# Attention units on one core: the transposes of a unit placed ahead of the product of the unit before it

## What is computed

```python
s = jnp.einsum('bqhd,bkhd->bhqk', qb, k) * scale
p = masked_softmax(s, pos[None, :] <= t[:, None])
return jnp.einsum('bhqk,bkhd->bqhd', p.astype(dt), v)
```

## Time and profile before

| | |
|---|---|
| median of 3 runs | 4166.8 us (4161.8 to 4168.43) |
| profiled execution | 4173.57 us, its span 4171.8 us |
| PE busy | 3686.4 us, 88% of the span |
| PEld busy | 2947.4 us, 71% |
| DVE busy | 2156.1 us, 52% |
| POOL busy | 1802.5 us, 43% |
| ACT busy | 1407.6 us, 34% |
| MLA, first layer | 248 to 306 us of the span |
| NSA, first layer | 346 to 450 us |
| Sparse, first layer of the second stack | 2494 to 2553 us |
| Fox, first layer of the second stack | 2553 to 2614 us |
| granted TensorE clock, mean | 0.905 of full speed |

### The profile page before, as it was taken

How to read it: one execution, slowest core, us unless ns; L and a number is a source line. 1 busy time by engine, 2 the same in 40 slices (tenths; PEclk the granted TensorE clock), 3 DMA queues, 4 the chain that set the end, 5 groups by cost and what they waited for, 6 DMA issues and landing times. The chain is left out here.

```text
span 4171.8 us, 48813 instructions
## 1 busy us (share of the span) xinstructions
PE 3686.4 (88%) x16148; PEld 2947.4 (71%) x16156; DVE 2156.1 (52%) x3077; ACT 1407.6 (34%) x2442; POOL 1802.5 (43%) x976
## 2 busy tenths in 40 slices
PE   7888899999888889999997778999998778999997
PEld 6755786787776657877786556877877566877876
DVE  4255497212243565962123475447863465547863
ACT  3234323322232352333222225323333225323332
POOL 3137553444340564443442447434543447434542
PEclk9877999999997689999998888999998888999998
DMA  3200122223321002222242110622233110622233
GB/s 117 71 11 1 61 96 76 85 96 131 123 77 65 0 1 81 90 81 86 89 144 101 51 61 1 242 81 81 96 131 110 49 61 1 242 81 84 97 136 116
DMA packets 99596, 354.89 MB, mean 85 GB/s; under 512 B 11888, under 2 KB 12528, under 8 KB 99312
## 3 DMA queue, kind: packets, MB, share of 16 engines
q1 hardware_dynamic: 99440, 352.94, 25.1%
HBM read 350.73 MB, written 2.10 MB: 85 GB/s over the span
## 5 line engine op out<-in xcount | busy, mean ns | idle before, releaser
L201 POOL TENSOR_TENSOR weights_lo<-arena,weights_hi 128x1024 fp32r<-128x1024 f32 x504 | 1288.5, 2558 | 1840.9 <-ACT weights_hi L195 1840.9
L263 PE MATMUL ps<-moving_hi,weights_hi 128*128 128x512 f32 x2752 | 720.7, 406 | 96.1 <-ACT weights_hi L195 38.0
L195 ACT ACTIVATE weights_hi<-arena 128x1024 fp32r<-128x1024 f32 x522 | 548.6, 1053 | 720.4 <-PE ps L414 403.2
L263 PE MATMUL ps<-moving_lo,weights_hi 128*128 128x512 f32 x2752 | 692.0, 393 | 2.4 <-DVE moving_lo L218 1.2
L263 PEld LDWEIGHTS ps<-moving_hi,weights_hi 128*128 128x128 f32 x2752 | 532.3, 194 | 223.5 <-issue 50.7
L263 PE MATMUL ps<-moving_hi,weights_lo 128*128 128x512 f32 x2752 | 686.0, 392 | 0.0
L263 PEld LDWEIGHTS ps<-moving_lo,weights_hi 128*128 128x128 f32 x2752 | 524.2, 190 | 117.9 <-DVE moving_lo L218 5.8
L263 PEld LDWEIGHTS ps<-moving_hi,weights_lo 128*128 128x128 f32 x2752 | 522.1, 190 | 109.6
L802 POOL TENSOR_SCALAR arena<-arena 128x128 f32<-128x128 f32 (+1 forms) x320 | 344.9, 1095 | 297.7 <-DVE arena L724 232.8
L1689 DVE SCALAR_TENSOR_TENSOR arena<-arena 128x1024 f32<-128x1024 f32 x128 | 188.3, 1483 | 421.5 <-DMA arena<-modw_first 344.7
L1573 DVE SCALAR_TENSOR_TENSOR arena<-arena 128x512 f32<-128x512 f32 x240 | 258.0, 1150 | 0.0
(11 more groups left out here) (298 smaller groups left out, 4542.9 us busy)
## 6 DMA issues: line engine op xcount, KB each, us to landing
arena<-wstream SPq DMA_DIRECT2D x532, 512.0 KB, 3.3
arena<-modw_first SPq DMA_DIRECT2D x64, 512.0 KB, 4.1
arena<-modw SPq DMA_DIRECT2D x64, 512.0 KB, 5.2
arena<-xT SPq DMA_DIRECT2D x1, 2048.0 KB, 8.7
outT<-arena SPq DMA_DIRECT2D x1, 2048.0 KB, 7.0
arena<-con SPq DMA_DIRECT2D x1, 1411.5 KB, 11.3
arena<-par SPq DMA_DIRECT2D x4, 136.0 KB, 3.1
arena<-arena SPq DMA_DIRECT2D x32, 2.0 KB, 1.7
```

What stands on the lines that cost most here:

```text
L195: m.nc.scalar.activation(m.w_hi[:, j % 2, :], slab(m, base + j), ACT.Copy).then_inc(hi_ready, 1)
L201: m.nc.gpsimd.tensor_tensor(m.w_lo[:, j % 2, :], slab(m, base + j), m.w_hi[:, j % 2, :].bitcast(F32), ALU.subtract)\
L263: mm = m.nc.tensor.matmul(bank, unit_tile(w, k), a[:, k, :], start=(p == 0 and k == 0), stop=(p == 2 and k == KD - 1))
```

## The change

In each round, TensorE's list now has the transposes of unit u between the scores of unit u+1 and the product of unit u-1. Before, they stood behind that product. No instruction is added or taken away, and the orders of the other engines are the same. It holds for all four kinds of attention.

```diff
--- before.py
+++ after.py
@@ -692,9 +692,9 @@
             for u in range(NU):
                 if u + 1 < NU:
                     score(u + 1)
+                turn(u)
                 if u:
                     product(u - 1)
-                turn(u)
             product(NU - 1)
```

## The result

The changed kernel takes 4266.61 us (median of four runs, 4263.66 to 4269.82) against 4164.3 for the kernel before (four runs, 4158.29 to 4168.43). The ratio is 1.0247, 95% interval 1.0229 to 1.0265: 102 us slower, where 100 was forecast. The span of the profiled execution went from 4171.8 to 4268.0.

The account below looks back on a forecast made before the run. ScalarE and VectorE handing over to each other bound the kernel (GpSimd in Sparse). Longer rings and stage ends +77 us and NSA's lower clock +23 gave +100, 4267 us, chance 0.48; own range 4250 to 4285, 8 in 10 4232 to 4302.

Parts of the forecast that it names:

- The ring of ScalarE and VectorE: In MLA before the change, ScalarE and VectorE waiting on each other set the pace, 5.82 us a unit; NSA 5.67.
- The new ring: After the change, a two-unit loop through scaling, transposes, product and ScalarE's copies: 12.95 us in MLA, 13.49 in NSA.
- The clock in NSA: Transposes and product of even NSA units run at the lower clock: +1.9 us a pair, +11.5 a stage.
- The ends: MLA's end: product(6) delays the last high parts by 2.1 to 3.8 us, a slow last product adds 1.1; +4.2 taken.
- Sparse: Sparse stage: the two-unit loop slightly exceeds GpSimd's pace, and the end costs more; 5 to 8 us, 6.5 taken.
- Fox: Fox stage: same unit as MLA, without weights and with one score term; 7.5 us longer.
- stages outside the attention would keep their lengths: Sign: stages after the attention keep their lengths, no growth.
- The even pace: MLA units come every 6.5 us, with TensorE idle 1.4 us before transposes; in Fox idle 1.4 to 2.2.
- The order does not matter: Rival: scaling always ends before the next unit's scores, so time stays within 8 us; no change, chance 0.04.
- faster: Rival: ScalarE's high copy finds all three transpose banks ready, saving perhaps half of 66.2 us; 4134, chance 0.03.
- The clock holds: Rival: TensorE's clock stays up in NSA and only the rings lengthen: +77 us, 4244; chance 0.20.
- The rival of falls in Sparse and Fox: Rival: the clock also falls about three times in each Sparse and Fox stage, +27 us above forecast, 4294; chance 0.18.

Follow-up runs that it names:

- The two edits on ScalarE: Changed kernel with the half copy behind the high parts: 4236.91 us; with two buffers for high and low parts: 4258.58; with both: 4165.9.
- the scaling runs: GpSimd scaling two of the four query tiles: on the changed kernel 4162.2 us, on the kernel before 4138.72 us.
- the run that makes it hold in NSA: Changed kernel with 11 added identity matmuls ahead of the transposes of every even NSA unit after the first: 4244.74 us.

## Why the prediction was right, point by point

- **What bounds the kernel.** The ring of ScalarE and VectorE, with TensorE and GpSimd outside, was right for the middle of the stages. The run with less scaling and the old order kept 5.8 us a unit. It was incomplete for the beginnings and ends, where GpSimd is on the path.
- **The new ring.** The sum of 12.95 for two units of MLA measured 12.91, and NSA's 13.49 measured 13.18 and 13.31 once the clock was held. The two edits on ScalarE show that it closes over both waits for the product, and the scaling runs show that GpSimd is in it.
- **The clock in NSA.** Idle 3.87 us (at least 3.5), low clock behind it, 1.7 us a pair for the 1.9 estimated. NSA grew by 27.0 and 26.0 for 28.5. That the total comes so near is partly two errors against each other. With the clock held the stages grew by 11.9 and 11.7, where I had 17: the pairs 13.2 to 13.3 and not 13.49, the first two units 0.6 shorter, the end 1.4 and not 2.5 to 4.5 longer. The clock then took 15.1 and 14.3 and not 11.5, since it slowed the end too.
- **The ends.** A rest of 2.1 to 3.8 and a slow last product were named; the last high parts of MLA came 3.6 us later behind their transposes (4.64 against 1.07). In MLA the time from the last reciprocal to the end of the stage grew by 4.2 and 3.6 for the 4.2 forecast, in Fox by 3.0. The run with the last unit alone gave 40 us in the timed runs and 33 in the span, for a range of 17 to 39.
- **Sparse**: 8.3 and 8.0 for 6.5. **Fox**: 4.5 and 4.4 for 7.5. Fox is the term that was mis-sized most. Its pairs did take 12.9 to 13.0 in the steady part, but the last reciprocal came 50.93 after the first matmul of the stage where it had been 49.48, so 1.45 and not 3.3. Its third reciprocal came 1.1 us earlier than before (18.80 after the first matmul instead of 19.89), because TensorE's clock rose 15.2 us after the first matmul there and not 20.1, and the first units follow TensorE. From the third reciprocal to the last it was 2.5 longer, which is the ring.
- **The moved wait hands something on.** I had said that stages outside the attention would keep their lengths. The compressed stage behind MLA grew by 1.7 and 1.9. The stage's stretch has a granted clock of 0.53 before and 0.50 after (the first field behind the five engines; the windows are of unequal length, and the clock is at the upper level only in the first 2.3 us of the first):

```profile
306.00:346.00 40.00, 34.07 (x112) 18.49 (x112) 11.37 (x18) 6.17 (x11) 31.49 (x32) 0.53 0.00 1
```

```profile
317.00:352.00 35.00, 29.47 (x102) 17.93 (x102) 10.20 (x15) 5.33 (x9) 31.15 (x32) 0.50 0.00 1
```

  MLA's last rows are at the lower clock now, and the next stage starts there. It isn't the order in MLA alone: with the new order in NSA only, the second layer's compressed stage took 42.7 us too, behind a MLA in the old order.
- **The even pace.** I had MLA's and Fox's units at an even 6.5 us, with 1.4 us idle on TensorE (in Fox 1.4 to 2.2). The second MLA stage and both Fox stages come near that: 6.1 to 6.8 us, with 1.1 to 1.5 idle. In the first MLA stage the units come in turns of 5.8 to 5.9 and 7.0 to 7.1, with 0.7 and 1.9 to 2.4 idle; the mean of a pair is the same. Nothing hung on it, since in the middle of these stages the clock held all the same.
- **The rivals.** "The order does not matter" and "faster" fell with the result. "The clock holds" gives 4244, and the run that makes it hold in NSA gives 4244.74. It was not what happened, and that the two agree to 1 us is luck: the stages of that run grew by 68 us in sum and not by 77, with NSA 5 a stage under and the compressed stage 2 a stage over. The rival of falls in Sparse and Fox came true in small part: in the first Sparse stage the transposes of units 4, 6 and 7 took 2.4 us, in the second those of 5 and 7, and in both Fox stages those of unit 6. Those of the last two units belong to the ends. That TensorE might run the product before the waiting transposes did not happen. The Trainium skill ("TensorE: Matmul & The Clock Gate", Part 1, on queue depths) says that TensorE's queue can pull weight loads ahead of matmuls in flight. In this trace the matmuls keep their order, and across a wait not even the first load runs ahead: it starts with its matmul, at 280.21 (the two rows in the last section).

That the total was off by less than 1 us is partly luck: over both layers Fox came out 6 us and NSA 4 under the forecast, the compressed stage 4, Sparse 3 and MLA 2 over it. The loss itself was 102 us for 100; the kernel before came out 2.5 us faster than the 4166.8 that the forecast starts from.

## What to carry to other kernels

Before an instruction that waits is moved ahead of one that is ready, ask who waits for the ready one. A wait that costs an engine nothing becomes a link in a ring as soon as another engine's work is queued behind it. Sum the ring over as many units as it spans and compare it with the present pace. If two instructions of one queue wait for the same event, removing either alone shows little, so remove both before the wait is called harmless. And where TensorE idles, the price is the idle time plus what runs slower after it; here 15 us in each of the two NSA stages.

## What the hardware showed that I had not expected

The idle piece just ahead of a matmul does not by itself tell which clock follows. The rows are from the changed kernel, first MLA, then Fox:

```profile
280.21 1.07 PEld L675 LDWEIGHTS ps<-arena 128*128 128x128 f32 x10 [2.75 <-POOL arena L802]
280.21 1.31 PE L675 MATMUL ps<-arena 128*128 128x128 f32 x10 [2.42 <-POOL arena L802]
```

```profile
2684.88 2.40 PE L675 MATMUL ps<-arena 128*128 128x128 f32 x10 [1.64 <-POOL arena L802]
```

After 2.42 us idle the transposes ran at 2.4 GHz, after 1.64 at 1.2 GHz. My reading of the earlier trace rows, longer than 1.94 us means slow, was too simple. In NSA it came true every time from the fifth unit on: there the piece in front of each even unit is 3.87 or 3.88 us long, and the transposes behind it took 1.81 to 2.40 us and not 1.31.

A matmul of the 128-column identity with itself in fp32 took 0.23 us at the upper clock, with two records each (26 are 52 records in 5.9 us), where a transpose of a 128x128 block of the same type takes 0.10.
